# Fixed weight buffers and tables of a two-block transformer kernel moved up by 96 bytes

## The reference

```
def _swiglu(h, w1, w3, w2):
    return (jax.nn.silu(h @ w1) * (h @ w3)) @ w2
...
merged = merged + jax.nn.sigmoid(h @ w_gate[l, i]) * (branches[i] @ w_branch[l, i])
...
x = x + merged @ w_out[l]
```

## Time and profile before

| | |
|---|---|
| median of 3 runs | 1864.07 us |
| the three runs | 1863.07, 1864.07, 1868.15 us |
| profiled execution, first to last instruction | 1858.3 us |
| TensorE matmul busy | 1815.3 us, 98% |
| TensorE weight load busy | 1567.5 us, 84% |
| VectorE busy | 1395.6 us, 75% |
| ScalarE busy | 1020.7 us, 55% |
| mean granted TensorE clock | 0.992 |
| read from memory | 360.39 MB |

### The profile page before, as it was taken

How to read it: one execution, slowest core, us unless ns; L and a number is a source line. 1 busy time by engine, 2 the same in 40 slices (tenths; PEclk the granted TensorE clock), 3 DMA queues, 4 the chain that set the end, 5 groups by cost and what they waited for, 6 DMA issues and landing times.

```text
span 1858.3 us, 29888 instructions
## 1 busy us (share of the span) xinstructions
PE 1815.3 (98%) x12638; PEld 1567.5 (84%) x12638; DVE 1395.6 (75%) x1520; ACT 1020.7 (55%) x1217; POOL 148.9 (8%) x161
## 2 busy tenths in 40 slices
PE   7999999999999999999999999999999999999999
PEld 7998898888899889788888888795888797668887
DVE  4988667857488966789999999875867574868674
ACT  5664345433565425477777777667433456765431
POOL 0021000212001200000000000000111000001110
PEclk9999999999999999999999999999999999799999
DMA  7422355453443235489999999644655344016461
GB/s 276 154 98 100 127 183 224 172 204 116 168 160 115 92 113 185 159 335 354 367 354 353 348 354 357 243 155 156 234 179 195 125 154 165 1 69 256 164 221 62
DMA packets 52266, 364.47 MB, mean 196 GB/s; under 512 B 5920, under 2 KB 6048, under 8 KB 9760
## 3 DMA queue, kind: packets, MB, share of 16 engines
q1 hardware_dynamic: 50832, 357.79, 51.8%
q0 software_dynamic: 1296, 4.72, 0.7%
HBM read 360.39 MB, written 2.10 MB: 195 GB/s over the span
## 4 chain that ended last, share of the span: by engine, by line
PE 60%; ACT 3%; DVE 3%; issue 1%; DVEq 0%; ACTq 0%
PE banks L1441 58%; ACT work L850 2%; PE banks L2102 1%; ACT h_parts L850 0%; PE banks L2366 0%; DVE h_parts L2540 0%; PE banks L2048 0%; DVE work L2870 0%; DVE work L2867 0%; DVE ring_lo L2483 0%; PE banks L1488 0%; ACT L850 0%; ACT scr L850 0%; PE banks L2360 0%; DVE small L3308 0%
## 5 line engine op out<-in xcount | busy, mean ns | idle before, releaser
L1441 PE MATMUL banks<-h_parts,high 128*128 128x256 f32 (+1 forms) x2576 | 554.8, 307 | 2.5 <-DVE h_parts L2540 1.5
L1441 PE MATMUL banks<-h_parts,ring_lo 128*128 128x256 f32 x1664 | 469.4, 282 | 0.0
L1441 PEld LDWEIGHTS banks<-h_parts,high 128*128 128x128 f32 x2576 | 417.6, 191 | 31.9 <-issue 9.8
L2483 DVE TENSOR_TENSOR ring_lo<-ring,high 128x2048 fp32r<-128x2048 f32 x154 | 352.7, 2298 | 67.9 <-ACT high L850 66.0
L850 ACT ACTIVATE high<-ring 128x2048 fp32r<-128x2048 f32 x154 | 292.4, 1904 | 68.7 <-DMA ring<-weights_in 65.3
L1441 PEld LDWEIGHTS banks<-h_parts,ring_lo 128*128 128x128 f32 x1664 | 317.4, 191 | 0.1
L850 ACT ACTIVATE work<-banks 128x512 f32<-128x512 f32 (+6 forms) x139 | 87.7, 636 | 258.9 <-PE banks L1441 252.8
L2483 DVE TENSOR_TENSOR more_lo<-more,more_high 128x2048 fp32r<-128x2048 f32 (+1 forms) x86 | 188.5, 2202 | 29.8 <-ACT more_high L850 29.7
L1441 PE MATMUL banks<-h_parts,more_high 128*128 128x512 f32 x592 | 207.3, 393 | 0.5 <-DVE h_parts L2540 0.5
L850 ACT ACTIVATE more_high<-more 128x2048 fp32r<-128x2048 f32 (+1 forms) x86 | 158.2, 1842 | 58.9 <-DMA more<-weights_in 58.9
L850 ACT ACTIVATE glu<-scr 128x256 f32<-128x256 f32 x66 | 27.6, 419 | 221.0 <-DVE scr L2507 221.0
(11 more groups left out here) (291 smaller groups left out, 3066.5 us busy)
## 6 DMA issues: line engine op xcount, KB each, us to landing
ring<-weights_in SPq DMA_DIRECT2D x225, 1024.0 KB, 4.9
more<-weights_in SPq DMA_DIRECT2D x104, 1024.0 KB, 5.5
more<-weights_in SPq DMA_DIRECT2D x8, 512.0 KB, 4.3
ring<-weights_in SPq DMA_DIRECT2D x6, 512.0 KB, 4.1
consts<-consts_in SPq DMA_DIRECT2D x1, 2034.0 KB, 17.2
params<-params_in SPq DMA_DIRECT2D x1, 1162.5 KB, 11.0
x<-x_in SPq DMA_DIRECT2D x2, 512.0 KB, 4.0
normed_rows<-scr POOLq DMA_DIRECT2D x2, 512.0 KB, 10.4
```

The source lines that it names most:

```text
L1441: return pe.matmul(out_, lhsT, rhs, start=start, stop=stop, **kw)
L2483: tt(lo_of(g), ring_of(g), hi_of(g).bitcast(F32), SUB).then_inc(unit_lo, 1)
```

## The change

A tensor of 24 float32, `align`, which nothing reads or writes, is made ahead of the raw buffers. Everything from `ring` to `crowded` thereby begins 96 bytes higher. The room is won back further on: `small` has 208 columns in place of 224 (columns up to 207 are used), and the two index tensors of one column are now one of two columns, so that `top_index` and all that follows it keep their places. `x`, `h_parts` and `scr`, which lie ahead of `align`, keep theirs. No instruction is added, removed or moved on any engine; the seven gathers of token rows on GpSimd read their indices from `row_indices`.

```
--- before.py
+++ after.py
@@ -428,15 +428,17 @@
         h_parts = sb("h_parts", [P, 2, KT, T], F32R)
         h_hi, h_lo = h_parts[:, 0, :, :], h_parts[:, 1, :, :]
         scr = sb("scr", [P, 2048])
+        sb("align", [P, 24])
         with ExitStack() as shared:
             ring_lo = shared.enter_context(nc.sbuf_tensor("ring_lo", [P, RING_FIXED, UNIT], F32R))
         ring = sb("ring", [P, RING_FIXED, UNIT])
         high = sb("high", [P, HIGH_FIXED, UNIT], F32R)
         consts = sb("consts", [P, N_CONSTS])
         params = sb("params", [P, N_PARAMS])
-        small = sb("small", [P, 224])
+        small = sb("small", [P, 208])
         crowded = sb("crowded", [P, 1], I32)
-        row_index = [sb(f"row_index{i}", [P, 1], U32) for i in range(2)]
+        row_indices = sb("row_indices", [P, 2], U32)
+        row_index = [row_indices[:, i:i + 1] for i in range(2)]
         rows = nc.dram_tensor("normed_rows", (T, D), F32, kind="Internal").ap()
         top_index = sb("top_index", [P, TT, 8], U32)
```

## The result

The changed kernel takes 1851.94 us (median of 8 runs, 1850.01 to 1855.39) where the kernel before has 1863.57 beside it; the ratio is 0.9949, 95% interval 0.9936 to 0.9963. The quotient of the two medians is 0.9938; the ratio with its interval compares fast runs with fast runs, and the text goes by it. Measured again later on another chip it was 1853.98 against 1859.34, ratio 0.9963 (0.9950 to 0.9975). Forecast were 1861.6 us, 0.13% less, and so no measurable change. The two ratios are 0.51% and 0.37%, about three to four times as much, and the range of 1855.5 to 1869.5 missed the time.

What follows compares the result with a forecast made beforehand. TensorE, busy 98% of the span, was taken as the bound; the terms -2.6 - 0.5 + 1.5 + 0.3 - 1.2 + 0 = -2.5 us gave 1861.6 us, 0.13% less, read as no change. The range was 1855.5 to 1869.5 us.

Steps and rivals of the forecast that it cites:

- What bounds the kernel: Whole span: TensorE, busy 98%; a nanosecond off a weight-stage matmul is one off the time; 5.8 us lie around the span.
- Engines beside TensorE at nothing: VectorE, ScalarE and DMA loads: no row that sees the address on VectorE or ScalarE, load gap taken as queueing; cost 0.
- Weights moving over `g`: Expert layer, `g_hi`/`g_lo` stationary: fixed weights reach the pace of upper ones, 5 to 6 ns each, 2.6 us faster.
- For `m`: Output projections, `m_hi`/`m_lo` stationary, 224 matmuls on fixed weights: between 0.2 and 1.1 us, taken as 0.5 us faster.
- Experts: Expert matmuls with `h_parts` stationary: fixed weights lose their same-place pace, 3 to 4 ns each, 1.5 us slower.
- The 0.3 us for 256 columns with `h_parts` stationary: 288 matmuls in six token-tile units: could lose part of the experts' 3 to 4 ns; at 1 ns, 0.3 us slower.
- Dense parts, 512 columns: Dense layers, `h_parts` moving: 208 matmuls at the slow 399 ns pace gain 6 ns each, 1.2 us faster.
- The mixers' 256 columns at 0: 3168 matmuls of mixers, gates and keys: 283 and 282 ns read as one pace, value 0; bounds 12.7 faster, 15.8 slower.
- Rival 2: Mixers, gates, keys, queries: 256-column matmuls pay for operands apart, 3.2 us at 1 ns, 1871.1 us at 3 ns; chance 0.13.
- Rival 3: Narrow 256-column matmuls gain up to 4 ns, 1852.1 us at 3 ns; chance 0.22, shared with several terms at upper end.
- Rival 1: All matmuls: place doesn't matter, the 3 to 6 ns are the stage's; 1864.1 us; chance 0.15 with losses up to 5.6.
- The clock: Attention near 1580 us: shifted work meets another clock level, 2.5 us either way, about 1859.1 or 1864.1; no separate chance.

Runs made afterwards that it cites:

- c_tables_only: Against the changed kernel, pad put behind `high`, so only `consts`, `params`, `small` and `crowded` move by 96 bytes: 1860.93 against 1860.12 us before, ratio 1.0008.
- F320: Against the changed kernel, `small` alone put ahead of `ring`, fixed weights at 320 bytes modulo 512: 1855.18 against 1859.88 us before, ratio 0.9973.
- F416: Against the changed kernel, `small` put with the pad ahead of `ring`, fixed weights at 416 bytes modulo 512: 1862.05 against 1860.12 us before, ratio 1.0008.
- F96: The changed kernel itself, fixed weights at 96 bytes from `x` modulo 512, 0 in the kernel before: 1851.94 against 1863.57 us, ratio 0.9949.
- a_tokens_too: Against the changed kernel, pad put ahead of `h_parts`, so tokens, fixed weights and upper buffers all lie at 96: 1853.46 against 1860.12 us before, ratio 0.9972.

## Why the prediction was wrong

*What bounds the kernel:* right. TensorE is busy 98% before and after, and what its matmuls lost, 11.8 us of busy time, came through as 9.5 us of span, with 2.3 us more of idle time. One reading beside it was wrong, without effect on the difference: in every execution of these kernels the time is 1.8 us over the span, not 5.8. The rest of the 5.8 was that the profiled execution was quicker than the median.

*Engines beside TensorE at nothing:* right, 2284 against 2283 ns on VectorE; 1917 against 1918 on ScalarE; the tables at nothing too, shown by c_tables_only.

*Weights moving over `g`:* right in sign, too small. 2.6 us were forecast from the fixed rows. They gave 146 x 6 + 146 x 6 + 202 x 6 = 3.0, and the upper rows another 294 x 2 + 294 x 1 + 238 x 1 = 1.1, which fits a matmul paying for its neighbour's place as well. This term was left out: 4.1 in all by row means, 4.6 by steps. For `m` 0.5 was taken; by steps the fixed rows fell by 4 to 7 ns and the upper by 3, 1.5 us together.

*Experts:* 1.5 us slower forecast, 264 x 2 + 180 x 6 = 1.6 measured, 1.9 by steps with the upper rows. The 0.3 us for 256 columns with `h_parts` stationary came to 0.1 by steps.

*Dense parts, 512 columns:* 399 to 392 on 208 matmuls is 1.5 us, 1.2 forecast; over all of them the steps of `h_parts,high` fell by 4.4 ns (464) and those of `h_parts,more_high` by 0.8 (592), 2.5 us. F320 has two paces at a place other than the tokens', so two paces are no mark of operands at one place.

*The mixers' 256 columns at 0:* this is the step that failed. It read `hb_hi` on `ring_lo`, 282 ns, as "operands apart" and 283 as "operands together", and took the agreement for a floor. But `hb` lies 96 above its weights and `h_parts` after the change lies 96 below, and the runs show these as unlike (283 and a step of 119.9 ns at F416, 281 and 118.1 at F96). Rival 2 named this very difference and put it only on the slower side. The measured gain per matmul is 2.7 ns near 44 us, (3.60 - 3.56) / 30 = 1.3 ns near 245 us, and 1.7 ns over all steps; on 3168 matmuls that is 5.4 us where 0 was forecast. By steps the terms sum to -5.4 - 4.6 - 1.5 + 1.9 + 0.1 - 2.5 = -12.0 us. With 2.3 us more of idle time and 1.9 us less by the clock the span would have fallen by 11.6; it fell by 9.5, and where the other 2 us went is open. Two rows at one value are no floor: F320 reached 113.3 ns in places.

*Rival 3* (1855.3 at 2 ns, 1852.1 at 3) is what happened, together with the larger `g` term. It had 0.22 with all that belonged to it. Rival 1, no dependence, falls with a_tokens_too: the same instructions, the weights at the same place as after, and a step of 119.84 ns against 118.14.

The rule of the Trainium skill that was weighed, separate read ports for the moving operand and the weight load ("TensorE: Matmul & The Clock Gate", step-by-step section), would have all rows alike. The 281 against 283 ns of one pair of buffers at two distances, on a kernel with equal order and waits, shows otherwise. Two ports may exist; the pace of the stream still depends on where both operands lie. That their reads meet somewhere in the memory would explain it, and no run here shows it.

*The clock* (rival 4) was priced at 2.5 us either way; two executions of the changed kernel differ by 0.003 of it, and of the 9.5 us between the two profiles it made 1.9.

## What to carry to other kernels

Where TensorE never waits, compare the steps of like matmuls over buffers at unlike addresses: a few ns each on thousands of matmuls were 0.4 to 0.5% here, for the price of a pad. In this kernel the place counted modulo 256, and the difference moving minus stationary with its sign; don't price one sign, or one value, by another. Judge by whole products and by many timed executions, compared at one granted clock: neighbours share the cost, and one profile's span moved by 7 us at unchanged paces.

## What was not expected of the hardware

- A stream of float32r matmuls of 256 columns ran at 120.0, 117.3 to 118.7 or 113.3 ns from start to start, by the difference of places of its operands modulo 256, and at two paces (113.3 and 117.7) at one and the same difference.
- The span of one and the same program goes with its granted clock: before the change, 1863.0 us at 0.988 (one execution), 1860.9 at 0.990, 1857.1 at 0.993 and 1856.2 at 0.994.
- Moving only the high parts (b_high_only) made a matmul quicker that reads none of them (`ring_lo,g_hi`, 395 to 393).
- VectorE (2283 and 2284 ns) and ScalarE (1918 and 1917) showed nothing of it with the same buffers.
